# The two memories arrive already transposed; their row scales are applied later

## The reference, cut to what matters

```
mem_n = rmsnorm(mem, norm_mem_w)                 # mem: 256 x 1024
kv    = mem_n @ xkv_w                            # keys and values, 1024 columns each
m2    = rms_norm(mem_2, mem_norm_g_2)
k2, v2 = m2 @ w_k_xa_2, m2 @ w_v_xa_2
rmsnorm(x, w) = x * rsqrt(mean(x * x) + eps) * w
# per head: softmax(q k^T / 16) v, with q from the tokens
```

## Time and profile before

| | |
|---|---|
| Median of 3 timed executions | 914.07 us (914.02 to 915.09) |
| Profiled execution, span from first to last instruction | 910.9 us |
| The same minus the median of the timed ones | -3.2 us |
| TensorE busy | 901.4 us, 99% |
| VectorE busy | 661.6 us, 73% |
| ScalarE busy | 504.2 us, 55% |
| GpSimd busy | 24.3 us, 3% |
| Data moved by DMA | 164.38 MB, 180 GB/s |

### The profile page before, as it was taken

The page is one execution under the profiler, slowest core; times in us unless marked ns, Lnnn a source line. Parts: engine busy times, 40 slices in busy tenths (PEclk is TensorE's granted clock), DMA queues, the critical chain, the costliest instruction groups (busy, mean ns, idle before and its releaser), DMA issues.

```text
span 910.9 us, 12836 instructions
## 1 busy us (share of the span) xinstructions
PE 901.4 (99%) x5160; PEld 787.4 (86%) x5160; DVE 661.6 (73%) x920; ACT 504.2 (55%) x584; POOL 24.3 (3%) x69
## 2 busy tenths in 40 slices
PE   9999999999999999999999999999999999999997
PEld 8888998889888888888888988888899888888886
DVE  5799999987577666656967996646686676565665
ACT  6796435655555444445656757744464654544444
POOL 1600010000000000000000000000000000000000
PEclk9999999999999999999999999999999999999999
DMA  9746555454355666654755455455453456666551
GB/s 353 253 159 223 183 199 185 139 185 140 92 186 186 195 199 197 190 185 153 238 188 183 159 166 183 152 175 187 173 185 103 144 183 191 196 193 197 189 185 47
DMA packets 101280, 164.38 MB, mean 180 GB/s; under 512 B 2736, under 2 KB 71088, under 8 KB 101104
## 3 DMA queue, kind: packets, MB, share of 16 engines
q1 hardware_dynamic: 100528, 161.71, 54.2%
q0 software_dynamic: 560, 1.84, 0.7%
q10 hardware_dynamic: 144, 0.16, 0.1%
HBM read 162.65 MB, written 1.05 MB: 180 GB/s over the span
## 4 chain that ended last, share of the span: by engine, by line
PE 92%; DVE 5%; DMA 2%; ACT 1%; issue 1%; SPq 0%; DVEq 0%; ACTq 0%
PE ps L609 20%; PE ps L611 19%; PE ps L610 19%; PE ps L646 18%; PE ps L650 9%; DVE w_lo L1719 1%; DVE c_acc L1865 1%; DMA w_ring<-in_w_in 1%; PE ps L737 1%; DMA head_raw<-in_head 1%; PE ps L857 0%; ACT w_hi L1227 0%; PE ps L774 0%; DVE mem_l L1734 0%; PE ps L826 0%
## 5 line engine op out<-in xcount | busy, mean ns | idle before, releaser
L1719 DVE TENSOR_TENSOR w_lo<-w_ring,w_hi 128x2048 fp32r<-128x2048 f32 x146 | 333.4, 2288 | 114.2 <-ACT w_hi L1227 113.2
L1227 ACT ACTIVATE w_hi<-w_ring 128x2048 fp32r<-128x2048 f32 x146 | 278.6, 1911 | 88.3 <-DMA w_ring<-in_w_in 27.3
L646 PE MATMUL ps<-xx,w_hi 128*128 128x512 f32 x720 | 171.8, 391 | 0.3
L646 PEld LDWEIGHTS ps<-xx,w_hi 128*128 128x128 f32 x720 | 133.3, 188 | 27.4 <-issue 0.7
L609 PE MATMUL ps<-w_hi,xx 128*128 128x512 f32 x304 | 120.2, 395 | 0.0
L611 PE MATMUL ps<-w_hi,xx 128*128 128x512 f32 x304 | 118.6, 390 | 0.0
L610 PE MATMUL ps<-w_lo,xx 128*128 128x512 f32 x304 | 118.5, 390 | 0.0
L650 PEld LDWEIGHTS ps<-xx,w_lo 128*128 128x128 f32 x720 | 92.3, 191 | 3.5
L650 PE MATMUL ps<-xx,w_lo 128*128 128x256 f32 x720 | 93.4, 283 | 0.0
L609 PE MATMUL ps<-w_hi,ff_h 128*128 128x512 f32 (+1 forms) x218 | 84.7, 389 | 0.0
L610 PE MATMUL ps<-w_lo,ff_h 128*128 128x512 f32 (+1 forms) x218 | 84.6, 388 | 0.0
(11 more groups left out here) (339 smaller groups left out, 1335.9 us busy)
## 6 DMA issues: line engine op xcount, KB each, us to landing
w_ring<-in_w_in SPq DMA_DIRECT2D x34, 1024.0 KB, 5.1
w_ring<-in_mlp_up_w SPq DMA_DIRECT2D x16, 1024.0 KB, 5.6
w_ring<-in_mlp_down_w SPq DMA_DIRECT2D x16, 1024.0 KB, 4.9
w_ring<-in_w_gate_ffn SPq DMA_DIRECT2D x11, 1024.0 KB, 5.3
w_ring<-in_w_up_ffn SPq DMA_DIRECT2D x11, 1024.0 KB, 5.3
w_ring<-in_w_down_ffn SPq DMA_DIRECT2D x11, 1024.0 KB, 4.9
w_ring<-in_xkv_w SPq DMA_DIRECT2D x8, 1024.0 KB, 5.4
w_ring<-in_w_out SPq DMA_DIRECT2D x8, 1024.0 KB, 4.8
```

The costliest lines, as they stand in the source:

```text
L646: pe.matmul(feat(bank + b), wh[:, k, b * P:(b + 1) * P], xx[:, k, :, :].rearrange("p e t -> p (e t)"), start=k == 0, stop=False)
L1227: act.activation(w_hi[:, s, :], w_ring[:, s, :], ACT.Copy).then_inc(hi_done, 1)
L1719: dve.tensor_tensor(w_lo[:, s, :], w_ring[:, s, :], w_hi[:, s, :].bitcast(F32), ALU.subtract).then_inc(lo_done, 1)
```

## The change

Two more inputs are prepared in DRAM, `mem_t` and `mem2_t`: the memories in transposed form. They are loaded next to the row forms, which are still needed for the squares. The high and low parts are made straight from SBUF without row scales. The 32 transposes, ScalarE's row multiplications and memory 2's place in the ring go away; all later slabs have a number one lower. The row scales of both memories are made on GpSimd. Values are multiplied by them when they leave PSUM (the row is the partition there). For keys the row is the free dimension, so the scales are written to a small DRAM tensor and read back as a row broadcast to all partitions (`r_row`); VectorE multiplies `kT` in two halves at the boundary into the first cross-attention, and `k2T` in one piece in the first MLP group. ScalarE's copies for the high parts of both key sets come behind these, and memory 2's low part follows `mlp1(0)`.

```diff
-I_M2 = 13
-I_V1 = (10, 11, 12, 14)
-I_K1, I_K2, I_V2 = 15, 19, 23
-I_OUT1 = 27
-I_Q1, I_O1 = 31, 35
-I_FF1 = 39
+I_V1, I_K1, I_K2, I_V2 = 10, 14, 18, 22
+I_OUT1 = 26
+I_Q1, I_O1 = 30, 34
+I_FF1 = 38
...
-        mem2_sq = at("mem2_sq", [P, 2, D], kv2 + 4 * D)
+        mem2_raw = at("mem2_raw", [P, KD, NMEM], split0)
+        mem2_tok = at("mem2_tok", [P, 2, D], split0 + 2 * D)
+        k2T = at("k2T", [P, KD, NMEM], kv2 + 2 * D)
...
+        mem_raw = at("mem_raw", [P, KD, NMEM], xn0)
...
+            sp.dma_start(mem_raw[:, :, :], a["mem_t"]).then_inc(mem_raw_loaded[0], 16)
+            sp.dma_start(mem2_tok[:, :, :], a["mem_2"].rearrange("a (t p) d -> p (a t) d", p=P)).then_inc(mem_loaded[1], 16)
-                    load(I_M2, a["mem_2"].rearrange("a (t p) d -> p (a t) d", p=P))
+                    sp.dma_start(mem2_raw[:, :, :], a["mem2_t"]).then_inc(mem_raw_loaded[1], 16)
...
+            def memory_row(n, r):
+                pool.wait_ge(mem_scales, n + 1)
+                row = a["scales"][n]
+                if n == N_MEM2:
+                    pool.wait_ge(scales_moved, 32)
+                pool.dma_start(row.rearrange("(t p) -> p t", p=P), r, allow_slow_non_contiguous=True).then_inc(scales_moved, 16)
+                if n == N_MEM2:
+                    pool.wait_ge(u_scaled, 2)
+                pool.wait_ge(scales_moved, 16 * (2 * n + 1))
+                pool.dma_start(r_row[:, 1 - n, :], row.partition_broadcast(P)).then_inc(scales_moved, 16)
             memory_scales(Q_MEM, r_mem)
-            pool.wait_ge(mem_scales, 1)
+            memory_row(N_MEM, r_mem)
...
             pool.wait_ge(dist_set, 1)
+            memory_scales(Q_MEM2, r_mem2)
+            memory_row(N_MEM2, r_mem2)
...
-            def memory_transpose(n, src, ms):
...
-            form_b_half(I_RV, 2, x_t, first_memory)
-            memory_transpose(N_MEM, mem_tok, (2, 3))
+            form_b_half(I_RV, 2, x_t)
+            pe.wait_ge(u_scaled, 2)
...
-                    memory_transpose(N_MEM2, w_ring[:, PLACE[I_M2], :].rearrange("p (t n) -> p t n", n=D), range(4))
...
-            def memory_rows(n, src, r):
...
             def memory_split_hi(n, dst, ks=range(KD)):
+                act.wait_ge(mem_raw_loaded[n], 16 * (n + 1))
...
-                    act.activation(dst[:, k, :], feat(memory_bank(n, k // 2))[:, (k % 2) * S:(k % 2 + 1) * S], ACT.Copy, scale=cols_g[:, c:c + 1]).then_inc(norm_hi, 1)
+                    act.activation(dst[:, k, :], (mem_raw, mem2_raw)[n][:, k, :], ACT.Copy, scale=cols_g[:, c:c + 1]).then_inc(norm_hi, 1)
...
                 raw_split_hi(n, 1)
+                if n == R_XA:
+                    act.wait_ge(ret_lo, 1)
+                    act.wait_ge(k_scaled, 2)
+                    act.activation(k_split[0][0][:, :, :], kT[:, :, :], ACT.Copy).then_inc(k_hi, 1)
                 hi(nxt + 2)
...
             act.wait_ge(dist_set, 1)
-            act.wait_ge(norm_sq, 2 * Q_MEM + 2)
+            act.wait_ge(norm_hi, KD)
+            act.wait_ge(norm_lo, KD)
             for hd in range(RET_HEADS):
...
+                act.wait_ge(mem_scales, b + 1)
+                r = (r_mem, r_mem2)[b]
...
+                        act.activation(v_split[b][0][:, m, half * HALF:(half + 1) * HALF], tok(2 * m + half), ACT.Copy,
+                                       scale=r[:, m:m + 1]).then_inc(v_ready, 1)
+            act.wait_ge(norm_lo, 2 * KD)
+            values(0, I_V1 + 3, (0,))
...
-            act.wait_ge(ret_lo, 1)
-            act.wait_ge(k_ready, 4)
-            act.activation(k_split[0][0][:, :, :], kT[:, :, :], ACT.Copy).then_inc(k1_hi, 1)
...
+                    act.wait_ge(k_scaled, 3)
+                    act.activation(k_split[1][0][:, :, :], k2T[:, :, :], ACT.Copy).then_inc(k_hi, 1)
...
+            def k1_scale(half):
+                f = slice(4 * half, 4 * half + 4)
+                dve.wait_ge(scales_moved, 32)
+                dve.wait_ge(k_ready, 4)
+                dve.tensor_tensor(kT[:, f, :], kT[:, f, :], r_row[:, 1, :].unsqueeze(1).broadcast_to([P, 4, S]), ALU.mult).then_inc(k_scaled, 1)
...
+                    if n == R_XA and tb == 0:
+                        k1_scale(0)
                     update_block(tb)
+                    if n == R_XA and tb == 0:
+                        k1_scale(1)
                     raw_split_lo(n, tb)
...
             conv(4)
             lo(12)
-            conv(2)
-            token_scales(Q_MEM2, r_mem2)
-            dve.sem_inc(mem_scales, 1)
-            conv(8)
+            conv(10)
+            memory_split_lo(N_MEM2, mem2_h, mem2_l, range(4))
+            lo(13)
+            conv(6)
+            memory_split_lo(N_MEM2, mem2_h, mem2_l, range(4, KD))
             lo(14)
-            conv(5)
-            memory_split_lo(N_MEM2, mem2_h, mem2_l, range(4))
+            conv(3)
+            value_rests(0, v1_lo, (0,))
             lo(15)
...
-            k_lo(0)
...
+                if first:
+                    dve.wait_ge(scales_moved, 64)
+                    dve.wait_ge(k_ready, 8)
+                    dve.tensor_tensor(k2T[:, :, :], k2T[:, :, :], r_row[:, 0, :].unsqueeze(1).broadcast_to([P, KD, S]), ALU.mult).then_inc(k_scaled, 1)
                 if splits:
                     for c in range(3):
                         lo(I_FF1 + 4 + c, step)
             mlp1(0, first=True)
+            dve.wait_ge(k_hi, 2)
+            dve.tensor_tensor(k_split[1][1][:, :, :], k2T[:, :, :], k_split[1][0][:, :, :].bitcast(F32), ALU.subtract).then_inc(k2_lo, 1)
             token_scales(Q_MLP, r_mlp)
```

More of the change, by code:

```diff
@@ L617, in form_a @@
             def form_a(i, banks, xt, n=256, step=0, ready=None, low_ready=None):
-                pe.wait_ge(lo_done, weight_count(i) + step)
+                pe.wait_ge(lo_done, i + 1 + step)
                 wh, wl = slab(i, n)
@@ L638, in form_a_pair @@
             def form_a_pair(i, bank, step=0, ready=(), low_ready=None):
-                pe.wait_ge(hi_done, weight_count(i) + step)
+                pe.wait_ge(hi_done, i + 1 + step)
                 wh, wl = slab(i, 256)
@@ L711, in form_b_half @@
                         between()
-            def memory_transpose(n, src, ms):
[L715 to L718, removed]
-                    for kk in range(2):
-                        f = 2 * m + kk
-                        for tb in range(TB):
-                            mm = pe.transpose(feat(memory_bank(n, m))[:, kk * S + tb * P:kk * S + (tb + 1) * P], src[:, tb, f * P:(f + 1) * P], ident[:, :])
-                    mm.then_inc(slab_used if n == N_MEM2 and m == 3 else norm_t, 1)
             def normed(n):
@@ L1313, in _ @@
             gate_sigmoid(1)
-            act.wait_ge(mem_loaded, 16)
-            act.wait_ge(mix_lo, KD)
-            norm_square(mem_tok, 0, Q_MEM)
-            norm_square(mem_tok, 1, Q_MEM)
+            act.wait_ge(mem_loaded[0], 16)
+            for tb in range(TB):
+                norm_square(mem_tok, tb, Q_MEM, mem_tok[:, tb, :])
             hi(6)
@@ L1367, in values @@
                     for half in range(2):
-                        act.activation(v_split[b][0][:, m, half * HALF:(half + 1) * HALF], tok(2 * m + half), ACT.Copy).then_inc(v_ready, 1)
-            values(0, I_V1[3], (0,))
+                        act.activation(v_split[b][0][:, m, half * HALF:(half + 1) * HALF], tok(2 * m + half), ACT.Copy,
+                                       scale=r[:, m:m + 1]).then_inc(v_ready, 1)
+            act.wait_ge(norm_lo, 2 * KD)
+            values(0, I_V1 + 3, (0,))
+            hi(15)
+            values(0, I_V1 + 3, (1,))
             hi(16)
-            values(0, I_V1[3], (1,))
-            hi(17)
             for j in range(4):
                 keys(I_K1, j, j % 2)
-                hi(18 + j)
+                hi(17 + j)
             keys(I_K2, 0, 0)
-            hi(22)
+            hi(21)
             act.wait_ge(ry_centred, 1)
@@ L1381, in _ @@
             keys(I_K2, 1, 1)
+            hi(22)
+            keys(I_K2, 2, 0)
             hi(23)
-            keys(I_K2, 2, 0)
-            hi(24)
             keys(I_K2, 3, 1)
@@ L1975, in _ @@
             ins.then_inc(ret_lo, 1)
+            lo(24)
+            conv(10)
             lo(25)
-            conv(9)
+            conv(len(order))
             lo(26)
-            conv(len(order))
-            lo(27)
             value_rests(1, v2_lo)
@@ L2436 @@
     data["head"] = np.concatenate([block.reshape(-1) for block in blocks])
+    for name in ("mem", "mem_2"):
+        data[name.replace("_", "") + "_t"] = data[name][0].T.reshape(KD, P, NMEM).transpose(1, 0, 2)
     data["w_spatial_t"] = np.asarray(inputs["w_spatial_2"])[0].transpose(0, 2, 1)
```

118 lines of the change are left out of this document (45 added, 73 removed).

## The result

The change makes the kernel slower, by 9.6 us where 3.6 were forecast: 923.63 us (median of 4 runs, 920.98 to 927.04) against 914.05 (912.85 to 915.09), ratio 1.011, 95% interval 1.0094 to 1.0125. The forecast was 917.7, range 915.6 to 919.2. The profiled run of the changed kernel took 923.95 us with a span of 922.2; before it was 910.9. The forecast had the sign right, and the size outside its range. One of the six executions of a later run, the one with the key copy moved at the boundary, took 1111 us at a mean granted clock of 0.75 and is left out of that run's median and range.

What follows compares the result with a forecast made beforehand. TensorE and VectorE were both taken as full from 40 to 65 us, TensorE alone after the cross-attention starts. Terms -0.6 + 1.15 + 3.05 = +3.6 us on 914.07 gave 917.7; 8-in-10 range 915.6 to 919.2.

Steps and rivals of the forecast that it cites:

- the row scales on GpSimd: Scales' trip through DRAM: landing 5.4 us as for a read, distances done at about 54.5, hidden with 6 us in hand.
- the three loads of a megabyte: Extra loads, net 2 MB more, go into stretches where the DMA share is 0.49; no cost given.
- The rival with the slow trip: From a landing of 11.5 us, late distances hold decay tables, `qkT` and `hi(11)`, so `lo(11)`: 919.9 us, chance 0.08.
- Memory 1, up to slab 10: TensorE's first 1.7 us are lost on VectorE; decay tables wait for `mem_l` until 60.7; slab 10 starts at 65.2 to 66.5.
- the upper case: Ahead of slab 10: `qkT` copies end at 66.4 instead of 65.1 if a table load stands behind the wait as well.
- the wait for `w_lo` at slab 11: TensorE's wait for `w_lo` at 71.4 was to be still there in the new profile.
- Memory 2, up to the first key slab: VectorE loses `token_scales`, filler is dealt out anew; TensorE gets slab 14 at 89.0 against 89.60: gain 0.6 us.
- the rule of the Trainium skill on the two sources: Fixed 120 cycles for PSUM, 58 for SBUF: 16 splits 1.0 us shorter; not adopted; as rival 917.1 us, chance 0.06.
- Boundary into the cross-attention: ScalarE's key copy ahead of the third query slab's `hi` delays VectorE's `lo` and TensorE's first scores: cost 1.15 us.
- First MLP group: Key work for `k2T` delays VectorE's group 1 by 4.15 us; TensorE waits 2.4 us, in all 3.05 us lost.
- The rest: Behind MLP group 1 all TensorE rows 3.6 us later than before, with no further difference to the end.
- The 3.2 us between span and median: Added to the 910.9 us span to get 914.07, to which the +3.6 us was added.

Runs made afterwards that it cites:

- the second measurement: The changed kernel run once more, unchanged, beside other runs on one chip: 922.33 us, ratio 1.0092.
- the run with the plain write: Changed kernel with each element-wise write of scales replaced by two whole rows of 512 bytes, keys getting ones as scales: 917.53 us, ratio 1.0037.
- the first of the three combined runs: Changed kernel with scales written once as 16-byte elements, decay tables early, MLP key splits and boundary key copy moved: 912.94 us, ratio 0.9995.

## Why the prediction failed, step by step

**The step that failed** is the one on the row scales on GpSimd. It ends with "Hidden, with 6 us in hand" and treats the write as something that one engine waits for. The question whom else a transfer delays was asked for the three loads of a megabyte, found harmless by their DMA share, and that was right (913.58). For the write it was not asked, as it has 1 KB. The landing was also misjudged: 9 to 13 us, not 5.4; the row is a read, and the nearest, but not near. The Trainium skill (DMA: Bandwidth & Descriptors, Rules for kernel authors) says that a non-contiguous last dimension becomes one descriptor per element, and advises a contiguous one; the landings of 10 against 4 us agree with the advice, and I had not weighed it. The descriptors themselves aren't seen: the trace has 16 packets of 64 bytes for the 256 elements and 16 of 128 bytes for the 128 larger ones. What such a write does to the loads of other queues only the runs here show. The rival with the slow trip had the landing as its condition, 11.5 us, and the decay tables as its path. With 11.3 us in the profiled run the distances were done at 60.45, just ahead of `mem_l`: by that path the trip would in fact have been hidden. In the second measurement, with a landing of 12.3 us, they were done at 61.51, and still the table load waited for something later: the `w_hi` of slab 10, done at 62.54 because its load was late. The cost came by that other path, the ring, ahead of slab 10 as well as at 106.

**What the step was worth.** By the run with the plain write, 923.6 or 922.3 less 917.5, so 5 to 6 us; by the write alone in the kernel before, 5.6.

**The clock.** No term of the sum has it. In the profiled run 1.7 us behind slab 10 and 3.0 behind the wait at 106 are TensorE at 1.2 GHz. The same wait of 2.46 us in the MLP was followed by such a stretch in four traces (the shift grew by 4.2 to 4.4) and not in two (3.4).

**Memory 1, up to slab 10:** right in places and causes. TensorE waited 0.7 us for `lo(9)`, 0.8 as a shift, where 1.2 were forecast; the decay tables started at 61.23 behind `mem_l`, with a table load behind the wait, as the upper case had it, and slab 10 at 66.96 (65.2 to 66.5 forecast). Part of what is beyond that is VectorE: `mem_l` took 1.91 us for four beside GpSimd's late distances, 1.65 in the earlier trace rows, and 1.67 in the run with the plain write, where the distances were done before. One sign failed: the wait for `w_lo` at slab 11 is gone, since TensorE gets there later than `w_lo` (with the plain write at 72.3 us).

**Memory 2, up to the first key slab:** -0.6 forecast, and -0.6 with the plain write by growth from 20 to 101 us (0.42 to -0.15); there TensorE started its first key slab at 89.37, where 89.0 was forecast. The splits took as long from SBUF as from PSUM, 1.67 and 1.65 us for four; the rule of the Trainium skill on the two sources (VectorE: DVE Perf Modes, section on the TRN2 errata) isn't borne out by this trace either.

```profile
85.56 1.67 DVE L1715 SCALAR_TENSOR_TENSOR mem_l<-mem_raw,cols,mem_h 128x256 fp32r<-128x256 f32 x4
```

**Boundary into the cross-attention:** +1.15 forecast, +0.9 in every trace that has the copy in its place, 0.0 with the copy moved. Right in place and cause.

**First MLP group:** +3.05 forecast. As waits 2.46 and 0.39, so 2.85; as shift 3.4 in the two traces where the clock held and 4.2 to 4.4 in the others. The mechanism is right, and the size nearly so where the clock held.

**The rest:** no difference was forecast behind the MLP, and +0.5 and +0.6 were measured, between 612 and 659 us, in two of the traces, beside waits of 0.38 and 0.49 us there, and not in others. Its cause is open.

**The 3.2 us between span and median.** They aren't all outside the first and last instruction, as the table of the time before says: one execution of the kernel before took 913.59 us with a span of 911.5, so 2.1 us lie outside; in the changed kernel it is 1.75 (923.95 and 922.2). The rest of the 3.2 was the difference between two executions. The sum uses only differences, and this one shifts it by 0.35.

So the forecast of 917.7 is near the time of the changed kernel with a harmless write, 917.5, and part of that is luck. By growth that trace has +4.4 us from 20 to 900: the early part came as forecast (-0.6), the stretch from 150 to 165 us won 0.4 that I had not counted, the boundary was 0.25 better, and the MLP took 4.4 instead of 3.05, as it held a stretch at the lower clock.

## What to carry to other kernels

Price a transfer by its elements and by what else is on the queues until it lands, not by its bytes: ask of each, as of each instruction, who stands beside it. A column of scalars that must become a row can be written in elements of 16 bytes, or turned on the chip first and written as a few rows; here the two came out alike (912.94 and 912.74 us). And where an engine is full, a wait of 2 us may cost 4: look for the granted clock behind each wait before taking its idle time for its price.

## What the runs showed of the hardware

- A DMA write of 256 elements of 4 bytes each from 128 partitions to DRAM landed after 9.0 to 12.9 us; 128 elements of 16 bytes after 3.6 to 4.2; two rows of 512 bytes after 3.8 and 5.5; 4 rows of 128 bytes after 2.7 to 3.9. Beside the first kind, ring loads of 1 MB on another queue landed after 7.3 to 16.8 us, where the kernel before has 5.2 to 7.8; with two such writes added to the kernel before, the queues moved 157 and 141 GB/s between issue and landing, against 184 and 262 in the same stretches without. Beside the others ring loads landed after 5.0 to 8.1 us.
- The packets of such a write of 4-byte elements were done 6.6 to 7.9 us before it landed (four writes, in the changed kernel and in the kernel before with the writes added); those of the writes of 16-byte elements and of rows 0.2 to 1.2 us before.
- The granted clock fell to the lower level at or behind nine of 16 waits of TensorE of 1.6 to 4.7 us in eight traces, at 1.5 to 3.0 us each (waits of 1.82, 2.20 and four of 2.46 us were among the nine; waits of 1.96, 3.07 and two of 2.46 us among the others), and once behind two short ones. Runs differ by it: at a mean clock of 0.998 the changed kernel took 920.98 us, at 0.990 927.04.
- In the first of the three combined runs (16-byte elements), a VectorE product that reads its second operand with a stride of 16 bytes took 2.02 us for 1024 elements, against 1.22 in the changed kernel for consecutive ones:

```profile
189.01 2.02 DVE L1769 TENSOR_TENSOR kT<-kT,r_row 128x1024 f32<-128x1024 f32 x1
```
